# First stage's x pieces: high and low parts of the rows in one 512-column product, a bank per block, halves added by VectorE at eviction

## The chip, the core and the metric

The kernel runs on one core of a Trainium2 chip. The metric is the device time of one execution in microseconds. [...] Each engine works through its own queue in order and meets the others at semaphores.

## The reference

One decoder layer over 2048 rows of width 1024, all in float32: RMSNorm, one input projection, two token mixers side by side, an output projection with residual, RMSNorm, a top-4-of-32 mixture of experts with residual, and a final RMSNorm. What the change touches is the part of the projection that feeds the convolution:

```python
h = rmsnorm(x, norm_mix_w[l])
proj = h @ w_in[l]                       # (2048, 1024) @ (1024, 3096)
q, k, v, g, a_low, z, xbc, dt_raw = jnp.split(proj, split_pts, axis=-1)
...
conv = lax.conv_general_dilated(xbc, ssd_conv_w[l][:, None, :], ...)   # 4 taps, per channel
xbc_act = jax.nn.silu((conv + ssd_conv_b[l]).astype(f32))
```

`xbc` has 1024 channels.

## The kernel before

The first stage, about the first 1030 us, takes the rows in eight rounds of 256 (s = 0 to 7); behind it the experts run in chunks. A float32 product is made of three: each operand is split into a high part (rounded to a narrower format, `fp32r` in the profile) and a low part (the rest), and high x high, high x low and low x high are summed in PSUM. For the rows the parts are `hhi` and `hlo`, for the weights the two halves of each of four buffers of `u2`.

The weights of a round come as 16 units of 1024 x 256 or 512 x 512. Units 0 to 3 are the x pieces (the channels of `xbc`), 4 to 11 the other columns of the input projection, 12 to 15 the output projection. In rounds 0 and 1 the raw unit is loaded, ScalarE makes its high part (`unit_hi`, L989), VectorE its low part (`unit_lo`, L1427), and both are stored to memory, from where later rounds load them ready. A unit's buffer is loaded again four units on, once TensorE is done with it.

An x piece (`x_piece`, L2045 to L2054) computes two blocks of 128 channels over the round's 256 rows. The weights are loaded into TensorE, the rows stream: for each block and each of 8 slices of the width, three products of 256 columns. Both blocks of a piece share one bank, columns 0 to 255 and 256 to 511. Piece n uses bank `pp[n % 2]`: x0 and x2 `pp0`, x1 and x3 `pp1`. `x_out` (ScalarE, L1000; the profile shows the copy under L941) copies the whole bank to `xT`, from where VectorE computes the convolution (`taps`). x2 starts when the copy of x0 is done, x3 when that of x1 is. Between the pieces TensorE does small work of the mixers; in round 0 there is little of it, and x1, x2 and x3 follow each other. After x3 come two small products into `pp0` (the gate step `zz`, L2244), which need the copy of x2, and a small transpose; VectorE then computes `dt0` and `zb` (`dt_zb`, L1532), and after `zb` the first product of unit 4 may start. It needs `pp0` and, for its second half, `pp1`, so the copy of x3.

The order of every engine's work is written out by hand in its `body(s, at)`; `at` is 0, 1, 2, 3 (a loop over rounds 3 to 5), 6 and 7. `rec` holds from round 1, `post` from round 2, `tx` up to round 6, `split` in round 0. `after(engine, step, n)` is a wait, `done` its signal. On ScalarE the copy of x3 follows `norm_sq(a + 3)` (L976), the sum of squares of an x tile that the next round needs and that is loaded during this one.

## Time and profile before

| | us |
|---|---|
| median of 3 runs | 3471.52 (3471.43 to 3477.55) |
| profiled execution, its own time | 3470.43 |
| its span | 3468.8 |
| TensorE busy in the span | 3405.6 (98%) |
| VectorE busy | 2140.4 (62%) |
| ScalarE busy | 1608.0 (46%) |
| x pieces (L2052), share of the chain that ended last | 5% |

The page gives busy time as shares of the span, which is the time from the first to the last instruction. Matmuls overlap: a row's duration is that of one product from start to end, and the pace of a run of them is the distance between starts. The granted clock (PEclk) of TensorE is 1.00 at 2.4 GHz and 0.50 at 1.2 GHz. In a row of the order of time, the number in brackets is how long the engine had stood idle before it, and what released it.

### The profile page before, as it was taken

To read this page: it belongs to the slowest core of one execution; us is meant where nothing else is said; L and a number is where in the kernel's file an instruction comes from. 1 tells how busy PE (TensorE), PEld (TensorE's weight loads), DVE (VectorE), ACT (ScalarE), POOL (GpSimd) and SP (SyncE) were. 2 spreads that over 40 slices of the span, in tenths; PEclk is the share of its full clock that TensorE was granted. 3 is DMA by queue.
4 is the path that set the end of the run, shared out by engine and by line. 5 is a ranking of instruction groups with operands and counts; after the bars stand their busy time and mean duration, and the time that the engine had idled before them with its cause. 6 is when DMAs were issued, how large, how long until landed. Compare 5 with 4: busy or idle time off the path is not lost.

```text
span 3468.8 us, 57452 instructions
## 1 busy us (share of the span) xinstructions
PE 3405.6 (98%) x21623; PEld 3101.2 (89%) x21623; DVE 2140.4 (62%) x2730; ACT 1608.0 (46%) x2045; POOL 630.0 (18%) x848
## 2 busy tenths in 40 slices
PE   7999999999999999999999999999999999999997
PEld 6888888888888999999999999988888888888986
DVE  4555455445456555555566666667777777777777
ACT  4443333333233444444444444455555555555555
POOL 1011111111113111111112112021112112212214
PEclk9999999999999999999999999999999999999998
DMA  9888887887876555555666656667667767767878
GB/s 377 346 321 322 302 288 286 303 300 284 300 254 192 168 165 166 184 182 181 184 192 198 194 181 202 188 206 242 208 212 218 245 214 229 246 223 229 252 241 307
DMA packets 475282, 826.58 MB, mean 238 GB/s; under 512 B 21837, under 2 KB 419293, under 8 KB 458784
## 3 DMA queue, kind: packets, MB, share of 16 engines
q1 hardware_dynamic: 443360, 721.83, 59.4%
q0 software_dynamic: 24320, 75.95, 9.6%
q10 hardware_dynamic: 7488, 27.27, 2.2%
q8 instruction: 73, 1.20, 0.1%
q14 instruction: 41, 0.34, 0.0%
HBM read 726.14 MB, written 98.96 MB: 238 GB/s over the span
## 4 chain that ended last, share of the span: by engine, by line
PE 92%; DMA 2%; DVE 2%; issue 1%; ACT 1%; POOL 0%; SPq 0%; POOLq 0%; DVEq 0%; ACTq 0%
PE pp L2062 14%; PE acc L2483 13%; PE acc L2479 11%; PE acc L2480 10%; PE acc L2481 10%; PE acc L2485 7%; PE pp L2052 5%; PE acc L2495 4%; PE acc L2497 4%; PE acc L2496 4%; PE tpm L2452 2%; PE tp L2031 2%; PE tpm L2458 1%; DMA uraw<-in_w_in 1%; PE seg L2107 1%
## 5 line engine op out<-in xcount | busy, mean ns | idle before, releaser
L1880 DVE TENSOR_TENSOR wlo<-raw,whi 128x2048 fp32r<-128x2048 f32 x384 | 876.0, 2289 | 298.5 <-ACT whi L1287 298.2
L1287 ACT ACTIVATE whi<-raw 128x2048 fp32r<-128x2048 f32 x384 | 730.3, 1910 | 149.1 <-PE acc L2497 102.7
L2483 PE MATMUL acc<-xhl,whi 128*128 128x512 f32 (+3 forms) x2304 | 762.9, 385 | 0.0
L689 POOL TENSOR_TENSOR gate_op<-gate_op 1x1 f32<-1x1 f32 x351 | 169.5, 483 | 2729.1 <-DVE ybuf L1918 533.4
L2485 PE MATMUL acc<-xhl,wlo 128*128 128x256 f32 (+3 forms) x2304 | 624.2, 271 | 0.0
L2479 PE MATMUL acc<-xhl,whi 128*128 128x272 f32 (+3 forms) x1792 | 534.9, 299 | 1.3 <-DVE xhl L1892 1.3
L2480 PE MATMUL acc<-xhl,whi 128*128 128x272 f32 (+3 forms) x1792 | 530.4, 296 | 0.0
L2481 PE MATMUL acc<-xhl,wlo 128*128 128x272 f32 (+3 forms) x1792 | 530.2, 296 | 0.0
L2483 PEld LDWEIGHTS acc<-xhl,whi 128*128 128x128 f32 x2304 | 431.9, 187 | 67.8
L2485 PEld LDWEIGHTS acc<-xhl,wlo 128*128 128x128 f32 x2304 | 437.3, 190 | 0.7
L2479 PEld LDWEIGHTS acc<-xhl,whi 128*128 128x128 f32 x1792 | 336.7, 188 | 1.5 <-issue 1.5
L2480 PEld LDWEIGHTS acc<-xhl,whi 128*128 128x128 f32 x1792 | 336.6, 188 | 0.0
L2481 PEld LDWEIGHTS acc<-xhl,wlo 128*128 128x128 f32 x1792 | 336.5, 188 | 0.0
L2062 PE MATMUL pp<-u,hhi 128*128 128x512 f32 x1024 | 325.8, 399 | 4.2 <-DVE zb L1411 4.2
L2479 PE MATMUL acc<-ahl,whi 128*128 128x272 f32 (+3 forms) x896 | 269.9, 301 | 0.0
L2481 PE MATMUL acc<-ahl,wlo 128*128 128x272 f32 (+3 forms) x896 | 265.4, 296 | 0.0
L2480 PE MATMUL acc<-ahl,whi 128*128 128x272 f32 (+3 forms) x896 | 265.3, 296 | 0.0
L2062 PEld LDWEIGHTS pp<-u,hhi 128*128 128x128 f32 x1024 | 190.3, 189 | 45.0 <-DVE zb L1411 4.3
L2495 PE MATMUL acc<-whi,ahl 128*128 128x512 f32 (+3 forms) x576 | 228.6, 397 | 1.1 <-DVE ahl L1946 1.1
L1320 ACT ACTIVATE ubuf<-acc,bgu 128x256 f32<-128x256 f32 (+7 forms) x200 | 86.6, 470 | 301.0 <-PE acc L2481 193.4
L2497 PE MATMUL acc<-whi,ahl 128*128 128x512 f32 (+3 forms) x576 | 225.3, 391 | 0.0
L2496 PE MATMUL acc<-wlo,ahl 128*128 128x512 f32 (+3 forms) x576 | 225.1, 391 | 0.0
(329 smaller groups left out, 5794.5 us busy)
## 6 DMA issues: line engine op xcount, KB each, us to landing
u<-split_d SPq DMA_DIRECT2D x112, 2048.0 KB, 8.9
raw<-in_moe_w_gate SPq DMA_DIRECT2D x128, 1024.0 KB, 4.8
raw<-in_moe_w_up SPq DMA_DIRECT2D x128, 1024.0 KB, 5.1
raw<-in_moe_w_down SPq DMA_DIRECT2D x128, 1024.0 KB, 9.4
split_d<-u SPq DMA_DIRECT2D x16, 2048.0 KB, 12.7
uraw<-in_w_in SPq DMA_DIRECT2D x12, 1024.0 KB, 10.7
yT<-in_moe_b_down SPq DMA_DIRECT2D x18, 512.0 KB, 12.2
xin<-in_x ACTq DMA_DIRECT2D x14, 512.0 KB, 8.6
```

Source lines behind the costliest of these rows:

```text
L1287: act.activation(whi[:, q % RING, :, :], raw[:, q % RING, :, :], ACT.Copy).then_inc(a_hi, 1)
L1880: dve.tensor_tensor(wlo[:, q % RING, :, :], raw[:, q % RING, :, :], whi[:, q % RING, :, :].bitcast(F32), ALU.subtract).then_inc(v_lo, 1)
L2052: m = pe.matmul(pp[n % 2][:, c * PW:(c + 1) * PW], w_[:, k, c * P:(c + 1) * P], h_[:, k, :], start=(k == 0 and w_ is wh and h_ is hhi), st ...
L2062: m = pe.matmul(pp[t][:, :], h_[:, 4 * q + k, :], w_[:, k, :], start=(q == 0 and k == 0 and h_ is th and w_ is wh), stop=(q == 1 and k == ...
L2479: pe.matmul(into[:, 0:n], hi_, of[:, k, 0, 0:n], start=(k == 0), stop=False)
L2480: pe.matmul(into[:, 0:n], hi_, of[:, k, 1, 0:n], start=False, stop=False)
L2481: m = pe.matmul(into[:, 0:n], lo_, of[:, k, 0, 0:n], start=False, stop=(k == KD - 1))
L2483: pe.matmul(into[:, 0:2 * n].rearrange("p (c n) -> p c n", c=2), hi_, of[:, k, :, 0:n], start=(k == 0), stop=False)
L2485: m = pe.matmul(into[:, n:2 * n], lo_, of[:, k, 0, 0:n], start=False, stop=(k == KD - 1))
L2495: pe.matmul(into, hi_, whi[:, slots_, k, :], start=(k == 0), stop=False)
L2496: pe.matmul(into, hi_, wlo[:, slots_, k, :], start=False, stop=False)
L2497: m = pe.matmul(into, lo_, whi[:, slots_, k, :], start=False, stop=(k == KD - 1))
```

## The change

`hhi` and `hlo` become the two halves of one tensor `hhl` (slice, part, row). One product streams both parts, 512 columns, against the high part of the weights into a whole bank: high x high in columns 0 to 255, low rows x high weights in 256 to 511. A second one of 256 columns adds high rows x low weights to the second half. Each of the two blocks now has a bank, block 0 `pp0`, block 1 `pp1`, in every piece. So a piece is 16 pairs of products in place of 16 triples, and it uses both banks. ScalarE copies the first half of each bank to `xT` (two copies of 256 columns), and VectorE (`x_sum`) adds the second half to it. Each block has steps of its own: x0a and x0, x1a and x1, and so on. A bank is free when VectorE's add is done, and every block of the next piece waits for that; `zz` and unit 4 wait for x3's.

```diff
     "act_sm": ["sm"],
-    "pe_x": ["x0", "x1", "x2", "x3"],
-    "act_x": ["x0", "x1", "x2", "x3"],
+    "pe_x": ["x0a", "x0", "x1a", "x1", "x2a", "x2", "x3a", "x3"],
+    "act_x": ["x0a", "x0", "x1a", "x1", "x2a", "x2", "x3a", "x3"],
+    "dve_x": ["x0a", "x0", "x1a", "x1", "x2a", "x2", "x3a", "x3"],
     "pe_zz": ["zz", "tdt"],
...
             hraw = pa("hraw", [KD, PW])
-            hhi = pa("hhi", [KD, PW], F32R)
-            hlo = pa("hlo", [KD, PW], F32R)
+            hhl = pa("hhl", [KD, 2, PW], F32R)
+            hhi, hlo = hhl[:, :, 0, :], hhl[:, :, 1, :]
             mT = pa("mT", [KD, P])
...
             def x_out(s, n):
-                after(act, f"pe_x.x{n}", s)
-                copy(xT[:, 2 * n:2 * n + 2, TAPS - 1:], pair_cols(pp[n % 2][:, :], 2), f"act_x.x{n}")
+                for c, step in enumerate((f"x{n}a", f"x{n}")):
+                    after(act, "pe_x." + step, s)
+                    copy(xT[:, 2 * n + c, TAPS - 1:], pp[c][:, 0:PW], "act_x." + step)
 
...
 
+            def x_sum(s, n):
+                for c, step in enumerate((f"x{n}a", f"x{n}")):
+                    after(dve, "act_x." + step, s)
+                    tt(xT[:, 2 * n + c, TAPS - 1:], xT[:, 2 * n + c, TAPS - 1:], pp[c][:, PW:], ALU.add, "dve_x." + step)
+
             def h_lo(s):
...
                     mix_ssd(a - 2)
+                x_sum(s, 0)
                 if tx:
...
                     ssd_add(a - 2)
+                x_sum(s, 1)
                 if post:
...
                     gla_decay(b)
+                x_sum(s, 2)
+                if rec:
                     gla_add(b)
+                x_sum(s, 3)
                 dt_zb(s)
...
                     mix_ssd(b)
-                after(dve, "act_x.x3", s)
+                after(dve, "dve_x.x3", s)
                 if rec:
...
 
-            def x_piece(s, n, at):
+            def x_piece(s, n, at, free, count):
 
...
                 wh, wl = unit_of(n, KD)
-                for c in range(2):
+                for c, step in enumerate((f"x{n}a", f"x{n}")):
+                    if free:
+                        after(pe, free[c], count)
+                    both = pp[c][:, :].rearrange("p (v n) -> p v n", v=2)
                     for k in range(KD):
-                        for w_, h_ in ((wh, hhi), (wh, hlo), (wl, hhi)):
-                            m = pe.matmul(pp[n % 2][:, c * PW:(c + 1) * PW], w_[:, k, c * P:(c + 1) * P], h_[:, k, :],
-                                          start=(k == 0 and w_ is wh and h_ is hhi), stop=(k == KD - 1 and w_ is wl))
-                done(m, f"pe_x.x{n}")
+                        pe.matmul(both, wh[:, k, c * P:(c + 1) * P], hhl[:, k, :, :], start=(k == 0), stop=False)
+                        m = pe.matmul(pp[c][:, PW:], wl[:, k, c * P:(c + 1) * P], hhl[:, k, 0, :],
+                                      start=False, stop=(k == KD - 1))
+                    done(m, "pe_x." + step)
 
...
                 after(pe, "dve_h.lo", s)
-                if post:
-                    after(pe, "dve_x2.a1", q)
-                elif rec:
-                    after(pe, "act_in.za", p)
-                x_piece(s, 0, at)
+                x_piece(s, 0, at, ("dve_x2.a1", "dve_x2.b1") if post else ("act_in.za", "act_in.zb") if rec else (),
+                        q if post else p)
                 if tx:
...
                     state(a - 2)
-                if post:
-                    after(pe, "dve_x2.b1", q)
-                elif rec:
-                    after(pe, "act_in.zb", p)
-                x_piece(s, 1, at)
+                x_piece(s, 1, at, ("dve_x.x0a", "dve_x.x0"), s)
                 if rec:
...
                     h2_turned(q * 2, 0)
-                after(pe, "act_x.x0", s)
-                x_piece(s, 2, at)
+                x_piece(s, 2, at, ("dve_x.x1a", "dve_x.x1"), s)
                 if rec:
...
                     gla_state(b, 1, p)
-                after(pe, "act_x.x1", s)
-                x_piece(s, 3, at)
+                x_piece(s, 3, at, ("dve_x.x2a", "dve_x.x2"), s)
                 if rec:
...
                 after(pe, "act_sm.sm", s)
-                after(pe, "act_x.x2", s)
+                after(pe, "dve_x.x3a", s)
                 for c in range(2):
...
                 after(pe, "dve_sp.zb", s)
-                first_half(s, 4, at, of_h, ("dve_sp.zb", "act_x.x3"), s)
+                first_half(s, 4, at, of_h, ("dve_sp.zb", "dve_x.x3"), s)
                 if rec:
...
                     cv_turned(1, p)
```

VectorE, opening round, from the scaling of the rows up to the splits of units 6 to 8, before (`u2` is a weight unit, `pp0` and `pp1` the banks):

```order
L1433 TENSOR_TENSOR hraw<-tp,cols 128x4x128 [waits dve_h,pe_tx,pe_sm,setup_a]
L1433 TENSOR_TENSOR hraw<-tp,cols 128x4x128
L1427 TENSOR_TENSOR u2<-uraw,u2 128x2048 [waits a_uh] x2
L1411 TENSOR_TENSOR dt0<-pm,shr 128x16 [waits pe_zz]
L1411 TENSOR_TENSOR zb<-pp0,shr 128x512
L1427 TENSOR_TENSOR u2<-uraw,u2 128x2048 [waits a_uh] x3
```

And of the changed kernel:

```order
L1435 TENSOR_TENSOR hraw<-tp,cols 128x4x128 [waits pe_tx,dve_h,pe_sm]
L1435 TENSOR_TENSOR hraw<-tp,cols 128x4x128
L1413 TENSOR_TENSOR xT<-xT,pp0 128x256 [waits act_x]
L1413 TENSOR_TENSOR xT<-xT,pp1 128x256 [waits act_x]
L1429 TENSOR_TENSOR u2<-uraw,u2 128x2048 [waits a_uh] x2
L1413 TENSOR_TENSOR xT<-xT,pp0 128x256 [waits act_x]
L1413 TENSOR_TENSOR xT<-xT,pp1 128x256 [waits act_x]
L1413 TENSOR_TENSOR xT<-xT,pp0 128x256 [waits act_x]
L1413 TENSOR_TENSOR xT<-xT,pp1 128x256 [waits act_x]
L1413 TENSOR_TENSOR dt0<-pm,shr 128x16 [waits pe_zz]
L1413 TENSOR_TENSOR zb<-pp0,shr 128x512
L1429 TENSOR_TENSOR u2<-uraw,u2 128x2048 [waits a_uh] x3
```

The adds of x1 stand ahead of the splits of units 4 and 5, those of x2 and x3 behind both.

ScalarE, round 2, from the second part of `qT` (mixer) to `dtl`, before (`xin` is the x tile that is loaded in this round):

```order
L1030 ACTIVATE qT<-tp 64x2x128
L941 ACTIVATE kT<-tp 128x256
L976 ACTIVATE junk,st<-xin 128x1024 [waits d_x,act_sq]
L941 ACTIVATE xT<-pp1 128x2x256 [waits pe_x]
L981 ACTIVATE xin<-xin,st 128x1024 [waits p_norm]
L957 DMA xres<-in_x 128x1024 [waits d_h20,pe_th]
L1120 ACTIVATE dtl<-dt0 128x16 [waits dve_sp]
```

And of the changed kernel:

```order
L1032 ACTIVATE qT<-tp 64x2x128
L942 ACTIVATE kT<-tp 128x256
L977 ACTIVATE junk,st<-xin 128x1024 [waits d_x,act_sq]
L942 ACTIVATE xT<-pp0 128x256 [waits pe_x]
L942 ACTIVATE xT<-pp1 128x256 [waits pe_x]
L982 ACTIVATE xin<-xin,st 128x1024 [waits p_norm]
L958 DMA xres<-in_x 128x1024 [waits d_h20,pe_th]
L1122 ACTIVATE dtl<-dt0 128x16 [waits dve_sp]
```

The copies of x3 are two now, at the same place behind the squares of the x tile.

TensorE, round 2, the end of x3 and the steps behind it, before:

```order
L2052 MATMUL pp1<-hlo,u2 128x256
L2052 MATMUL pp1<-hhi,u2 128x256
L2244 MATMUL pp0<-w_up,smT 128x256 [waits act_x,act_sm,act_rec]
L2244 MATMUL pp0<-w_up,smT 128x256
L2248 MATMUL pm<-ident,smT 128x24 x2
L2137 MATMUL pg<-qT,kT 128x128 [waits dve_g,act_qk]
L2137 MATMUL pg<-qT,kT 128x128 x3
```

And of the changed kernel:

```order
L2066 MATMUL pp1<-hhl,u2 128x512
L2067 MATMUL pp1<-hhl,u2 128x256
L2250 MATMUL pp0<-w_up,smT 128x256 [waits dve_x,act_sm,act_rec]
L2250 MATMUL pp0<-w_up,smT 128x256
L2254 MATMUL pm<-ident,smT 128x24 x2
L2152 MATMUL pg<-qT,kT 128x128 [waits dve_g,act_qk]
L2152 MATMUL pg<-qT,kT 128x128 x3
```

The gate step (`w_up`) waits for VectorE's add of x3's block 0 (`dve_x`) where it waited for ScalarE's copy of x2 (`act_x`).

## Rows read from the trace of the kernel before

**Rows 1.** Busy time by stretch: PE, PEld, DVE, ACT, POOL (count), PEclk, DMA share, GB/s.
```profile
325.00:450.00 125.00, 125.00 (x744) 108.18 (x743) 60.76 (x142) 42.91 (x87) 17.96 (x31) 1.00 0.82 293
```

**Rows 2.** In order of time (start, duration, us): TensorE, x0 of round 5.
```profile
633.56 0.28 PE L2052 MATMUL pp<-hlo,u 128*128 128x256 f32 x1
...
638.95 0.28 PE L2052 MATMUL pp<-hlo,u 128*128 128x256 f32 x1
```

**Rows 3.** In order of time, TensorE, expert stage, pairs 1 and 16.
```profile
2499.63 0.40 PE L2483 MATMUL acc<-xhl,whi 128*128 128x512 f32 x1
2499.87 0.28 PE L2485 MATMUL acc<-xhl,wlo 128*128 128x256 f32 x1
...
2504.93 0.40 PE L2483 MATMUL acc<-xhl,whi 128*128 128x512 f32 x1
```

**Rows 4.** In order of time, TensorE, 512-column products of a row unit.
```profile
583.57 0.39 PE L2062 MATMUL pp<-u,hlo 128*128 128x512 f32 x1
...
588.37 0.40 PE L2062 MATMUL pp<-u,hlo 128*128 128x512 f32 x1
```

**Rows 5.** In order of time, a 256-column copy and a 256-column VectorE operation.
```profile
151.43 0.39 ACT L941 ACTIVATE kT<-tp 128x256 f32<-128x256 f32 x1
...
121.85 0.41 DVE L1411 TENSOR_TENSOR cbm<-pm,m_le 128x256 f32<-128x256 f32 x1
```

**Rows 6.** In order of time, VectorE, opening round.
```profile
56.05 2.29 DVE L1427 TENSOR_TENSOR u<-uraw,u 128x2048 fp32r<-128x2048 f32 x1 [6.39 <-ACT u L989]
58.26 0.17 DVE L1411 TENSOR_TENSOR dt<-pm,shr 128x16 f32<-128x16 f32 x1
```

**Rows 7.** In order of time, ScalarE, opening round.
```profile
48.09 0.60 ACT L941 ACTIVATE xT<-pp 128x512 f32<-128x512 f32 x1 [0.76 <-PE pp L2052]
54.11 1.91 ACT L989 ACTIVATE u<-uraw 128x2048 fp32r<-128x2048 f32 x1 [5.42 <-DMA uraw<-in_w_in]
```

**Rows 8.** In order of time, TensorE, opening round.
```profile
33.10 1.97 PE L2031 MATMUL tp<-ident,xin 128*128 128x128 f32 x8 [3.97 <-ACT xin L981]
...
53.74 1.13 PE L2244 MATMUL pp<-w_up,smT 16*128 16x256 f32 x4
...
59.17 1.19 PE L2062 MATMUL pp<-u,hhi 128*128 128x512 f32 x2 [4.22 <-DVE zb L1411]
```

**Rows 9.** Busy time by stretch, after the two pauses of the opening round.
```profile
36.00:38.00 2.00, 2.00 (x11) 2.00 (x11) 0.49 (x1) 0.00 (x0) 0.00 (x0) 0.50 0.98 410
38.00:39.00 1.00, 1.00 (x9) 1.00 (x8) 0.00 (x0) 0.00 (x0) 0.00 (x0) 0.84 1.03 442
...
62.00:63.00 1.00, 1.00 (x6) 0.80 (x5) 0.00 (x0) 1.00 (x1) 0.00 (x0) 0.89 0.92 387
```

**Rows 10.** The page's DMA issues: KB each, us to landing.
```profile
uraw<-in_w_in SPq DMA_DIRECT2D x12, 1024.0 KB, 10.7
```

**Rows 11.** In order of time, TensorE, the wait for the ramp.
```profile
85.84 3.55 PE L2107 MATMUL seg<-ramp,m_gt 128*128 128x512 f32 x4 [2.33 <-DVE ramp L1411]
```

**Rows 12.** In order of time, ScalarE, round 2.
```profile
267.12 0.60 ACT L941 ACTIVATE xT<-pp 128x512 f32<-128x512 f32 x1 [0.42 <-ACT xres L1062]
...
284.43 1.06 ACT L976 ACTIVATE junk<-xin 128x1024 bf16<-128x1024 f32 x1 [8.76 <-DMA xin<-in_x]
...
285.49 0.58 ACT L941 ACTIVATE xT<-pp 128x512 f32<-128x512 f32 x1
```

**Rows 13.** In order of time, TensorE, round 2, x2's first product and zz.
```profile
267.98 0.36 PE L2052 MATMUL pp<-hhi,u 128*128 128x256 f32 x1
...
280.96 1.12 PE L2244 MATMUL pp<-w_up,smT 16*128 16x256 f32 x4
```

**Rows 14.** In order of time, ScalarE then TensorE, round 6.
```profile
788.32 1.06 ACT L976 ACTIVATE junk<-xin 128x1024 bf16<-128x1024 f32 x1 [2.09 <-DMA xin<-in_x]
789.28 0.19 ACT L976 ACTIVATION_READ_ACCUMULATOR junk<-xin 128x1 f32 x1
...
791.51 1.13 PE L2244 MATMUL pp<-w_up,smT 16*128 16x256 f32 x4
```

## The prediction

> **What bounds the kernel now.** I read the busy time by stretch first, then TensorE's and the other engines' rows in order of time around the x pieces (units 0 to 3 of a round; x0 to x3 below, rounds numbered s = 0 to 7). From round 3 on TensorE never stands still: 125.00 of 125.00 us busy at full clock, with VectorE busy 60.76 and ScalarE 42.91 [rows 1]. There a microsecond of TensorE is a microsecond of the run, and work for the other two is free as long as TensorE never waits for it. The opening round is another stage: TensorE waits for VectorE and ScalarE, which wait for weight units to land and be split [rows 6 to 8]. So three questions decide: how much shorter is a piece, do the new adds come before TensorE wants the bank, and where does a queue ahead of them stand still?
>
> **What the products give.** A piece had 16 triples of 256 columns; between the second product of one x0 and the same product 15 triples later lie 638.95 - 633.56 = 5.39 us, 0.3593 us a triple [rows 2]. It gets 16 pairs, 512 and 256 columns. The expert stage runs this very pair: 15 of them from 2499.63 to 2504.93, 0.3533 us each [rows 3]. That is 0.006 us a pair, 0.10 us a piece. The other bound is built from single forms: 21 products of 512 columns in 588.37 - 583.57 = 4.80 us, 0.2286 each [rows 4], plus a third of the triple, 0.1198, gives a pair of 0.3484 and 0.17 us a piece. I take the pair as it stands in the trace. 24 pieces (rounds 1 and 3 to 7) count, since those of rounds 0 and 2 end in a wait (below): -2.3 us, with -4.2 and 0 as ends.
>
> The Trainium skill, "TensorE: Matmul & The Clock Gate", section "Back-to-back issue gap", gives an isolated matmul columns / 2.4 GHz plus about 2.5 ns. By it dropping one product of three at equal columns saves 2.5 ns a pair, an estimate of 1.0 us for 24 pieces. The trace's 256 columns take 119.8 ns where that rule says 109, so it does not hold here, and the sum would change by 1.3 us only.
>
> **What the evictions cost.** Each piece now has two 256-column copies on ScalarE (such a copy out of PSUM takes 0.39 us, a 512-column one 0.60) and two 256-column adds on VectorE (0.41 us for one that reads PSUM) [rows 5, 7]. That is 64 x 0.39 - 32 x 0.60 = 5.8 us more ScalarE and 64 x 0.41 = 26 us more VectorE over eight rounds, spread over engines half idle [rows 1]: nothing by itself. That the high and low parts of the rows now lie side by side in memory changes no instruction's length or count, and I cost it at nothing. What it moves is the release of the banks. Before, piece n+2 waited for the copy of piece n, a whole piece (5.8 us) in between. Now half c of piece n+1 waits for copy and add of half c of piece n, with one half piece (2.8 us) and the small work between. Copy, add and two hand-overs take about 0.39 + 0.41 + 0.1 = 0.9 us, so in a quiet round it fits. In front of the adds, however, stand whatever VectorE and ScalarE have in their queues.
>
> **Opening round, the first stall.** On VectorE the order is now: adds of x1, splits of units 4 and 5, adds of x2. The split of unit 5 starts at 56.05, released by ScalarE's half of it at 54.11, which waited 5.42 us for the unit to land; it ends at 58.26 [rows 6, 7]. Before, x3 went into the other bank and ran without a pause after x2 (x2's copy is at 48.09 [rows 7], so x2 ends near 47.8). Now x3 needs x2's first add, done at 58.26 + 0.41: it starts at about 58.75 and TensorE has stood 11 us. Behind the late adds queue the decay inputs (dt0, zb) and the splits of units 6 and 7; behind x3 the load of unit 7, which takes its place.
> After such a pause the granted clock is at its lower level (0.50). After 3.97 us of waiting, work resumed at 33.10 and was at half clock until about 38.3; after 4.22 us, from 59.17 to about 62.2 [rows 8, 9]. So 3.0 to 5.2 us at half clock, 1.5 to 2.6 lost. x3: 16 x 0.3533 + 2.1 = 7.75, to 66.5. The small products behind it last from 53.74 to 54.95 (59.17 less its wait), 1.2 us: 67.7. From the start of dt0's row to the first product of unit 4 it took 59.17 - 58.26 = 0.9: 68.6 in place of 59.17, +9.4 [rows 6, 8]. The pause that was there, and its 1.5 us of half clock, go: +8.0 (7.4 to 8.5). Unit 7 is loaded only once x3 is done, at 66.5; 10.7 us to land [rows 10] and some 4 us to be split put it in place at 82, and TensorE, with three units of 5.5 us each (24 x 0.2286) before it, wants it at 85: in time, by 3 us. All later loads of the round are issued as TensorE frees units, so they move along, and so does TensorE's wait for the ramp (2.33 us at 85.84) [rows 11]. Nothing takes the 8 us back, since from round 3 on TensorE has no slack.
>
> **Round 2, the second stall.** ScalarE's copies of x3 stand behind the squares of the next x tile, which waited 8.76 us for its landing, to 284.43; the x3 copy started at 285.49 [rows 12]. That hurt nobody: the next user of pp0, the two-product gate step (zz), needed only x2's copy and ran at 280.96 [rows 13]. Now zz needs x3's first half copied and added: 285.49 + 0.39 + 0.41 + 0.06 = 286.35, +5.4 us, and the pause lowers the clock again, 1.5 to 2.6 us, I take 2.0: +7.4. In the same round x2's first half needs x1's add: copy at 267.12 [rows 12], free at 268.0, against a start at 267.98 [rows 13]: +0.1. In the other rounds with such a tile it lands earlier: in round 6, the tightest, the squares end at 789.47, so bank 0 is free at 790.4, and zz runs at 791.51 [rows 14]; 1.1 us to spare.
>
> **Sum.** 8.0 + 7.4 + 0.1 - 2.3 = +13.2 us. The profiled execution took 3470.43 us (span 3468.8), so 3483.6 by its own time; the median of the runs, 3471.52, lies 1.1 higher: **3484.7 us**. The measurement tells 0.2%, 6.9 us, from no change.
>
> **Rivals.**
> 1. The x tile of round 2 lands in time, over 5.5 us earlier than before. Only the first stall stays: 8.0 - 28 x 0.10 = +5.2, 3476.7. For it: in round 6 that wait is 2.09 us and not 8.76 [rows 14]. Against: the traffic of round 2 is issued by TensorE's own pace and shifts with it.
> 2. Not slower: the pause of round 0 lets the DMA queues get 8 us ahead. It decides from the point where unit 9 and round 2's x tile land some 4 and 6 us sooner after their issue: then the ramp wait (2.3 + 1.5 for its clock) goes and the second stall too: 8.0 - 3.8 - 2.8 = +1.4, 3472.9. Against: the loads are issued only when TensorE frees a place, so there is little to run ahead with.
> 3. The adds never hold TensorE (unit 5's wait absorbed, zz not held): -32 x 0.10 = -3.2, with the other bound -5.6: 3466 to 3468. This would need VectorE to reach x2's adds before 47.8, ahead of a split it has in front of them in its queue; nothing in the trace speaks for it.
> 4. More stalls: tiles landing over 1.1 us later in rounds 3 to 6, where there is as little to spare as in round 6, or half-piece waits that break TensorE's stream 32 times. At 3 us a round for four rounds +12: 3497.
>
> **Chances.** Forecast 0.62 (its own range 3480 to 3489, from 1.1 either way on the clocks, 2 us either way on the landing, 2 on the products); rival 1 0.14, rival 2 0.06, rival 3 0.04, rival 4 0.14. The forecast, rival 4 and the top of rival 1 are slower by over 0.2% (above 3478.5): 0.79. The rest of rival 1 and rival 2 are within it: 0.17. Rival 3 counts as faster: 0.04, though only its far end nears the limit. Range 3476 to 3491: it takes in rival 1 and leaves out rivals 2 and 3 and most of 4.
>
> **What would show it.** In round 0 x3's first product at 58 to 59 us, released by VectorE's add, with the clock at 0.50 behind it; unit 4's first product 9 us later than before. In round 2 a wait of 5 us before the gate step, released by an add. Pieces of about 5.7 us in place of 5.8. From round 3 on every round as long as before less 0.4 us. The forecast is wrong if x3 follows x2 in round 0 without a pause, or if rounds 3 to 7 show waits of TensorE for VectorE.

## The result, and the profile after

In all rows PE is TensorE and PEld its weight loads, ACT is ScalarE, DVE is VectorE, POOL is GpSimd and SP is SyncE; ACTq stands for a transfer (DMA) that ScalarE issues.

The change makes the kernel slower. The median of 4 runs is 3502.66 us (3496.22 to 3509.59), that of the kernel before 3471.69 (4 runs); ratio 1.0087, 95% interval 1.0075 to 1.0099. Forecast were +13.2 us and 3484.7, in a range of 3476 to 3491. The sign was right, the size too small by 18 us. The profiled execution took 3509.59 us (span 3507.9), 39 us more than the profiled one before.

TensorE's three waits that are new or longer in the first stage, in the profile after (engine, tile, line; what it waited for: us in total, times, longest):

```profile
PE pp L2250 <- DVE xT L1413: 12.1, 3, 4.6
PE pp L2066 <- DVE xT L1413: 11.6, 1, 11.6
PE seg L2122 <- DVE ramp L1413: 3.8, 1, 3.8
```

Two of these were forecast, and one of the two came three times: the gate step (L2250) waits for an add in rounds 2, 3 and 4. In order of time, TensorE in the opening round (x3, unit 4, the ramp), in answer to [rows 8, 11]; then the gate step of rounds 1 to 5, in answer to [rows 13, 14]:

```profile
58.48 0.77 PE L2066 MATMUL pp<-hhl,u 128*128 128x512 f32 x1 [11.63 <-DVE xT L1413]
68.88 6.37 PE L2077 MATMUL pp<-u,hhl 128*128 128x512 f32 x27 [0.96 <-DVE zb L1413]
95.61 3.78 PE L2122 MATMUL seg<-ramp,m_gt 128*128 128x512 f32 x4 [3.83 <-DVE ramp L1413]
...
169.28 1.13 PE L2250 MATMUL pp<-w_up,smT 16*128 16x256 f32 x4
297.57 2.04 PE L2250 MATMUL pp<-w_up,smT 16*128 16x256 f32 x4 [4.57 <-DVE xT L1413]
433.72 2.07 PE L2250 MATMUL pp<-w_up,smT 16*128 16x256 f32 x4 [3.42 <-DVE xT L1413]
570.71 2.07 PE L2250 MATMUL pp<-w_up,smT 16*128 16x256 f32 x4 [4.15 <-DVE xT L1413]
703.29 1.13 PE L2250 MATMUL pp<-w_up,smT 16*128 16x256 f32 x4
```

In rounds 6 and 7 the gate step stands at 830.40 and 956.45, with no wait. The distance between gate steps is the length of a round. In the kernel before they stand at 157.10, 280.96, 408.61, 536.26, 663.92, 791.51 and 918.24 in rounds 1 to 7:

| | to round 1 | 1 to 2 | 2 to 3 | 3 to 4 | 4 to 5 | 5 to 6 | 6 to 7 |
|---|---|---|---|---|---|---|---|
| before | 157.10 | 123.86 | 127.65 | 127.65 | 127.66 | 127.59 | 126.73 |
| after | 169.28 | 128.29 | 136.15 | 136.99 | 132.58 | 127.11 | 126.05 |
| difference | +12.2 | +4.4 | +8.5 | +9.3 | +4.9 | -0.5 | -0.7 |

They sum to +38.2 of the 39 us. A wait lengthens the round that ends with it, and what it costs afterwards falls into the next one. The windows behind the wait of round 4 show why (from:to, length, busy time of PE, PEld, DVE, ACT and POOL with counts, granted clock of TensorE, DMA share, GB/s):

```profile
568.00:570.00 2.00, 0.00 (x0) 0.00 (x0) 0.00 (x0) 1.22 (x3) 0.00 (x0) 0.78 0.87 328
570.00:572.00 2.00, 1.29 (x3) 1.10 (x4) 0.75 (x2) 1.38 (x3) 0.89 (x3) 0.50 1.00 369
576.00:578.00 2.00, 2.00 (x11) 2.00 (x11) 0.00 (x0) 0.00 (x0) 0.00 (x0) 0.50 0.08 31
580.00:582.00 2.00, 2.00 (x6) 1.52 (x6) 1.30 (x3) 0.62 (x1) 0.00 (x0) 0.50 0.00 0
582.00:584.00 2.00, 2.00 (x9) 1.59 (x8) 1.22 (x3) 0.71 (x3) 0.00 (x0) 0.81 0.00 0
584.00:586.00 2.00, 2.00 (x11) 1.63 (x10) 0.30 (x1) 0.00 (x0) 0.00 (x0) 1.00 0.00 0
```

A wait of 4.15 us, and TensorE, busy all the time afterwards, runs at 1.2 GHz until about 583. What it does there are the small products behind the gate step, at half speed:

```profile
572.86 2.08 PE L2152 MATMUL pg<-qT,kT 128*128 128x128 f32 x8
574.73 3.46 PE L2197 MATMUL pm<-rw,mT 128*128 128x32 f32 x16
578.00 1.95 PE L2043 MATMUL tp<-ident,mixed 128*128 128x128 f32 x8
```

In the kernel before, at full clock in the same round:

```profile
537.41 1.16 PE L2137 MATMUL pg<-qT,kT 128*128 128x128 f32 x8
538.40 1.87 PE L2182 MATMUL pm<-rw,mT 128*128 128x32 f32 x16
540.11 1.07 PE L2031 MATMUL tp<-ident,mixed 128*128 128x128 f32 x8
```

What made the waits of rounds 3 and 4 is in ScalarE's rows. After, round 3 and then round 4: the expert-stage input of the second token tile (`xres`, L1064), which waits until the store of that tile (`xacc_d<-xres`) is done, behind it the issue of the x tile, then the squares, which wait for its landing, and in round 4 the two copies of x3 behind them:

```profile
415.11 1.15 ACT L1064 ACTIVATE xres<-xres,sto 128x1024 f32<-128x1024 f32 x1 [6.12 <-DMA xacc_d<-xres]
...
417.05 0.37 ACTq L946 DMA_DIRECT2D xin<-in_x  x1
...
431.79 1.06 ACT L977 ACTIVATE junk<-xin 128x1024 bf16<-128x1024 f32 x1 [6.63 <-DMA xin<-in_x]
...
548.74 1.15 ACT L1064 ACTIVATE xres<-xres,sto 128x1024 f32<-128x1024 f32 x1 [3.37 <-DMA xacc_d<-xres]
...
550.70 0.36 ACTq L946 DMA_DIRECT2D xin<-in_x  x1
...
568.78 1.06 ACT L977 ACTIVATE junk<-xin 128x1024 bf16<-128x1024 f32 x1 [7.35 <-DMA xin<-in_x]
569.74 0.19 ACT L977 ACTIVATION_READ_ACCUMULATOR junk<-xin 128x1 f32 x1
569.84 0.64 ACT L942 ACTIVATE xT<-pp 128x256 f32<-128x256 f32 x2
```

And in the kernel before, round 4:

```profile
519.44 0.42 ACTq L945 DMA_DIRECT2D xin<-in_x  x1
532.26 1.06 ACT L976 ACTIVATE junk<-xin 128x1024 bf16<-128x1024 f32 x1 [1.25 <-DMA xin<-in_x]
```

In round 4 the squares begin 18.1 us after the issue where it was 12.8, and the issue itself comes 1.0 us later ahead of the gate step. In round 3 the larger part is the issue. The kernel before issued that tile at 391.79, 16.8 us ahead of its gate step; after, it is issued 13.3 us ahead of the moment at which the gate step would have run without its wait (433.72 - 3.42), because `xres` in front of it waited 6.12 us for its store where it had waited 2.41. From issue to squares it then took 14.7 us, which was 13.0 before. So the tile comes late in two ways: its issue stands behind another transfer in ScalarE's queue, and its own landing takes longer. I had read the spare time of all later rounds from the one landing of round 6 [rows 14]. The trace before already had more than one value, 13.0, 12.8, 12.5 and 13.8 us in rounds 3 to 6, and 17.3 in round 2.

### The profile page after: what moved, and what is told of

It is laid out like the page before. It is cut to its first block, busy times and chain, and to the rows that moved or that the text cites. A ratio compares the mean times of both kernels' runs of the same rounds, so it can differ in the third digit from the quotient of the medians.

```text
span 3507.9 us, 56534 instructions
## 1 busy us (share of the span) xinstructions
PE 3424.2 (98%) x21111; PEld 3093.7 (88%) x21111; DVE 2165.8 (62%) x2794; ACT 1612.2 (46%) x2077; POOL 641.0 (18%) x848
## 4 chain that ended last, share of the span: by engine, by line
PE 89%; DMA 5%; DVE 3%; issue 1%; ACT 1%; POOL 0%; SPq 0%; ACTq 0%; POOLq 0%; DVEq 0%
PE pp L2077 13%; PE acc L2489 13%; PE acc L2485 10%; PE acc L2486 10%; PE acc L2487 10%; PE acc L2491 6%; PE acc L2501 4%; PE acc L2503 3%; PE acc L2502 3%; PE pp L2066 2%; PE tpm L2458 2%; PE tp L2043 1%; DMA xin<-in_x 1%; DMA xacc_d<-xres 1%; DMA uraw<-in_w_in 1%
## 5 line engine op out<-in xcount | busy, mean ns | idle before, releaser
L690 POOL TENSOR_TENSOR gate_op<-gate_op 1x1 f32<-1x1 f32 x351 | 186.5, 531 | 2761.2 <-DMA xacc_d<-ybuf,tabb 521.1
L2077 PE MATMUL pp<-u,hhl 128*128 128x512 f32 x1536 | 374.2, 401 | 1.0 <-DVE zb L1413 1.0
L2077 PEld LDWEIGHTS pp<-u,hhl 128*128 128x128 f32 x1536 | 290.5, 191 | 63.8 <-issue 2.9
```

Source lines behind the costliest of these rows:

```text
L690: pool.tensor_tensor(gate_op[0:1, 0:1], gate_op[0:1, 1:2], gate_op[0:1, 1:2], ALU.add).then_inc(gate_ran, 1)
L2077: m = pe.matmul(pp[t][:, :], h_[:, 4 * q + k, :], w_[:, k, :], start=(q == 0 and k == 0 and h_ is th and w_ is wh), stop=(q == 1 and k == ...
```

## The experiments

Each kernel was compared with runs of the kernel before on the same chip (medians of that one: 3476.21 beside e1 to e4, 3474.03 beside e5 to e8, 3472.72 beside e9 to e11, 3475.68 beside e12). The theories are these. Theory of the queues: all of the loss is TensorE waiting for adds and copies that stand behind other work in the queues of VectorE and ScalarE, and the low clock behind each wait. Rival: the adds, the finer hand-over and their PSUM traffic cost by themselves.

| kernel | us | ratio to before, 95% |
|---|---|---|
| e1_x2_adds_first | 3487.33 | 1.0029 (1.0018 to 1.0039) |
| e2_x3_half_first | 3488.02 | 1.0034 (1.0020 to 1.0047) |
| e3_both | 3483.04 | 1.0020 (1.0011 to 1.0029) |
| e4_gate_wait_alone | 3494.74 | 1.0056 (1.0040 to 1.0071) |
| e5_x3_ahead | 3472.08 | 0.9993 (0.9984 to 1.0002) |
| e6_x1_ahead_too | 3471.39 | 0.9994 (0.9985 to 1.0003) |
| e7_all_orders | 3467.68 | 0.9982 (0.9973 to 0.9991) |
| e8_no_adds | 3468.87 | 0.9992 (0.9983 to 1.0001) |
| e9_before_orders | 3471.09 | 0.9997 (0.9988 to 1.0007) |
| e10_ramp_ahead | 3464.82 | 0.9981 (0.9972 to 0.9990) |
| e11_before_ramp_ahead | 3468.62 | 0.9989 (0.9980 to 0.9998) |
| e12_opening_as_changed | 3481.40 | 1.0016 (1.0007 to 1.0025) |

### x2's adds ahead of the split of unit 5

```diff
                 if split:
                     unit_lo(4)
-                    unit_lo(5)
...
                 x_sum(s, 2)
+                if split:
+                    unit_lo(5)
```

> Changed kernel with one edit: in the opening round VectorE adds x2's halves ahead of the split of unit 5. Theory (the loss is two kinds of waits of TensorE, each with its stretch at half clock): the 11.6 us wait before x3 goes; the gate step now waits for x3's add, which stands behind that split, so first products of unit 4 start near 61 us in place of 68.9. About 8 to 10 us less than the changed kernel's 3502.7, near 3493; the waits of the gate step in rounds 2 to 4 stay. Rival (64 adds and the traffic they make slow every round a little): under 2 us gained.

Measured 1.0029. In the profiled run x3's wait of 11.6 us is 2.83, but round 2 keeps its stall, and round 7 has one of another kind: x2 waits for x1's add, whose copy stands on ScalarE behind work that waits for a transfer (`xacc_d`).

```profile
49.93 0.47 PE L2067 MATMUL pp<-hhl,u 128*128 128x512 f32 x1 [2.83 <-DVE xT L1413]
...
288.11 2.04 PE L2251 MATMUL pp<-w_up,smT 16*128 16x256 f32 x4 [5.77 <-DVE xT L1413]
...
919.25 0.77 PE L2067 MATMUL pp<-hhl,u 128*128 128x512 f32 x1 [4.33 <-DVE xT L1413]
```

So every place where an add or copy follows a transfer in a queue is a place where TensorE can now stall.

The gain was twice what I expected. The kernel is 11.1 us slower than the one before, where the change as it stands is 31.0 slower: 20 us gained by an edit of the opening round alone, 8 to 10 expected. The expectation said that the waits of rounds 3 and 4 stay. In this profile they are gone (rounds 3 to 6 show no wait at the gate step), though ScalarE's order, the products and the adds are as in the changed kernel, and though round 2 stalls for longer, 5.77 us. So a stall in round 2 does not by itself bring those of rounds 3 and 4. In round 3 the tile is again issued late, 13.8 us ahead of the gate step, but its squares begin 10.3 us after the issue, where it was 14.7. The stalls of rounds 3 and 4 hang on the landing as much as on the issue, and one edit elsewhere was enough to lose them. The gains of the edits can therefore not be added up.

### The first half of x3 ahead of the squares; and both edits

```diff
+                x_out(s, 3, (0,))
                 if tx:
...
                     norm_sq(a + 3)
-                x_out(s, 3)
+                x_out(s, 3, (1,))
```

> Changed kernel with one edit: ScalarE copies the first half of x3 ahead of the squares of the x tile that it waits for, in every round. Theory: the gate step never waits for VectorE's add in rounds 2 to 6, each such wait with the stretch at half clock behind it is gone: near 3479 to 3482 us, 20 less than the changed kernel, and runs that differ less from each other. The opening wait of 11.6 us stays, with some 9 us of cost against the kernel before. Rival (the adds themselves): no more than 4 us gained.

> Both edits, of the opening round and of the gate step. Theory: only the shorter products stay, 0.4 to 0.6 us a round in seven rounds, against some 1.5 us of the gate step's wait in the opening round: 3468 to 3471 us, level with the kernel before (3471.7) or up to 0.1% faster. Rival (adds and copies cost by themselves): 3480 us or more.

Measured 1.0034 and 1.0020. The first gains 19 us against the change as it stands, close to the 20 expected. Both together are a miss: level with the kernel before was expected, and at 6.8 us slower the number is the one that the rival had named. The profile tells why. The gate step no longer waits for the tile, but in round 2 the wait moves a few products on: VectorE's add of x3's second half waits for the copy behind the squares, and dt0 is queued behind that add. In both runs TensorE stands over 3 us in round 2, and the clock falls again. Both edits together, TensorE and then VectorE:

```profile
289.92 3.52 PE L2200 MATMUL pm<-rw,mT 128*128 128x32 f32 x16 [3.35 <-DVE dt L1415]
```

```profile
289.36 0.42 DVE L1415 TENSOR_TENSOR xT<-xT,pp 128x256 f32<-128x256 f32 x1 [6.92 <-ACT xT L942]
289.70 0.17 DVE L1415 TENSOR_TENSOR dt<-pm,shr 128x16 f32<-128x16 f32 x1
```

From round 2 to 3 it takes 133.85 us, then 126.87, 126.86 and 127.02. The loss is one wait that the edit left in place, in round 2, and not a little in every round.

### The gate step's wait alone, in the kernel before

```diff
-                after(pe, "act_x.x2", s)
+                after(pe, "act_x.x3" if at >= 2 else "act_x.x2", s)
```

> Kernel before with one edit: from round 2 on the gate step waits for ScalarE's copy of x3 and not of x2; products, banks and evictions as before. Theory: the copy stands behind the squares of the late x tile, so round 2 has a wait of some 5 us before the gate step and over 10 us at half clock behind it, 9 to 11 us of cost, and rounds 3 and 4 may follow as they did in the changed kernel: 3481 to 3500 us. Were the later waits (rounds 3 and 4) due to the new products or the adds, only round 2 shows one and the time is near 3481. Rival (the wait is harmless, the clock comes back at once): 3476 us.

Measured 1.0056, +18.5 us, with no other part of the change in it, in the range expected. The profiled run, gate steps of rounds 2 to 4:

```profile
287.93 2.04 PE L2244 MATMUL pp<-w_up,smT 16*128 16x256 f32 x4 [5.61 <-ACT xT L941]
421.45 1.13 PE L2244 MATMUL pp<-w_up,smT 16*128 16x256 f32 x4 [0.69 <-ACT xT L941]
549.87 1.13 PE L2244 MATMUL pp<-w_up,smT 16*128 16x256 f32 x4 [0.69 <-ACT xT L941]
```

From round 2 to 3 lie 133.52 us, where a round is 127.65 before. The wait in round 3 accounts for 0.69, so 5.2 us were lost after the wait was over. Windows of the same run, behind the wait of round 2 and in round 5:

```profile
290.00:292.00 2.00, 2.00 (x12) 1.96 (x10) 0.77 (x2) 1.44 (x4) 0.00 (x0) 0.50 0.59 234
...
298.00:300.00 2.00, 2.00 (x8) 1.59 (x8) 0.59 (x2) 1.34 (x3) 0.00 (x0) 0.79 0.00 0
300.00:302.00 2.00, 2.00 (x11) 1.65 (x10) 1.45 (x3) 0.00 (x0) 0.00 (x0) 1.00 0.00 0
...
680.00:684.00 4.00, 4.00 (x27) 4.00 (x26) 1.68 (x8) 1.47 (x3) 0.00 (x0) 0.64 0.98 412
684.00:688.00 4.00, 4.00 (x13) 3.32 (x12) 2.42 (x7) 1.34 (x3) 0.00 (x0) 0.51 0.40 166
```

From the end of the wait at 287.9 to about 299 it is at half clock. The short waits of 0.69 us mostly cost their own length: round 3 to 4 takes 128.42, 0.77 more than before. But in round 5, behind such a short one, the clock fell too, for part of 680 to 688, and that round took 131.66, 4.1 more. It fell again behind the short wait of round 7 (0.50 from 942 to 946). So the low clock here belongs to a late gate step, but not only to waits of several us.

Of the three stalls only that of round 2 comes back here. The expectation had left it open whether rounds 3 and 4 follow, and taken one large wait alone as a sign that those two come from the products or the adds. The kernel e1_x2_adds_first speaks against that: it has the products and the adds, and no stall in rounds 3 and 4 either. What e4 shows is the price of a wait at this place, 5.61 us and 5.2 of clock, without anything else of the change.

### Both copies of x3 ahead; x1 and the x tile ahead too; the adds left out

```diff
+                x_out(s, 3)
                 if tx:
...
                     norm_sq(a + 3)
-                x_out(s, 3)
```

(with the edit of x2's adds). The second kernel adds, on ScalarE:

```diff
                 if post:
-                    for t in range(2):
-                        h2_of(q, t)
-                        h2_out(q, t)
+                    h2_of(q, 0)
+                    h2_out(q, 0)
                 x_out(s, 1)
                 if tx:
                     x_in(a + 3)
+                if post:
+                    h2_of(q, 1)
+                    h2_out(q, 1)
```

The third is the first without `x_sum`, every `dve_x` wait turned into `act_x`; the sum of the halves is left out.

> The changed kernel with VectorE's adds of x2 ahead of the split of unit 5 (opening round) and both of ScalarE's copies of x3 ahead of the squares of the x tile (all rounds). Theory of the queues (all of the loss is TensorE waiting behind other work in the queues of VectorE and ScalarE, and the half clock behind each wait): the first half of this order, with only one copy moved, left one wait in round 2 (logits, 3.4 us) and a pitch 133.85 from round 2 to round 3 against 127.65; with both copies moved that wait goes, every round from 3 on is 0.5 to 0.7 us shorter than before, and the run is within 2 us of the kernel before. Rival (the adds or the shared banks cost TensorE by themselves, through half pieces that wait and PSUM traffic): the loss stays at +5 or more though no wait over 1 us is left in rounds 2 to 7.

> As the kernel with x3's copies ahead, and in ScalarE's queue x1's copies and the load of the x tile stand ahead of the second token tile's expert-stage input (h2_of of tile 1), which waits for a transfer. Theory of the queues: the x tile's load is issued within 0.3 us of its place coming free in every round (it was 3.5 us in rounds 2 and 3), so that its landing no longer varies, and the scatter between runs shrinks to that of the kernel before (6 us between fastest and slowest, at most); 0 to 2 us faster than the kernel with x3's copies ahead. Rival (the landing varies with the DMA queues and not with the issue): no difference in time, and the squares still wait 6 us or more for the tile in round 2; since nobody waits behind them any more this costs nothing either.

> The kernel with x3's copies ahead, with VectorE's 64 adds left out (the low parts of the product are computed by TensorE and never added) and with all waits on the adds turned into waits on ScalarE's copies. What it measures is the price of the adds and of the hand-over to VectorE. Theory of the queues: only in the opening round does TensorE wait for an add, so this is 1 to 4 us faster than the kernel with x3's copies ahead, and from round 3 on each round is as long as there. Rival (the adds cost by themselves, through PSUM traffic or short waits at each half piece): each round is 0.5 us or more shorter here, 5 us or more in all.

Measured 0.9993, 0.9994 and 0.9992. With x3's copies out of the tile's way, and x2's adds ahead of the split, the loss of 31 us is gone. The adds cost nothing that can be measured: 64 adds more or less change the time by less than some 4 us. Round 3 to 4 and 4 to 5 take 126.97 and 126.87 us with them, 126.87 and 126.87 without. At 0.5 us or more a round the rival falls. Moving x1 and the tile too did not change the time: in one profile it took away a wait of 1.8 us in round 3 (round 2 to 3: 128.97, then 126.87), and the scatter did not shrink (7.5 us and 8.9 us from fastest to slowest), against what I expected.

### All orders in the opening round

```diff
                 if split:
+                    x_sum(s, 2, (0,))
                     unit_lo(4)
-                    unit_lo(5)
+                    x_sum(s, 2, (1,))
...
                 x_sum(s, 3)
                 dt_zb(s)
                 if split:
+                    unit_lo(5)
```

(ScalarE's copies likewise.)

> As the kernel with x1's copies ahead too, and in the opening round the copies and adds of x2 and x3 and the decay inputs (dt0, zb) stand ahead of the split of unit 5 (x2's first half ahead of that of unit 4). Theory of the queues: x3 follows x2 with a pause of under 3 us, the gate step behind it; unit 4's first product starts near 55.6 in place of 59.17 in the kernel before, and 5 us ahead of the kernel with x1's copies ahead; whether unit 5 then comes in time decides what of that is kept: between -5 and -1 us against the kernel before, 3471 to 3475 if that one is at 3476. Rival: the splits of units 4 to 7 and their stores move back by as much, unit 5 is waited for, and the gain against the kernel with x1's copies ahead is under 1 us.

Measured 0.9982 (0.9973 to 0.9991): faster than the kernel before by 3 to 9 us, by 6.4 in the medians where 1 to 5 was expected. x3 follows x2 with no wait of note, unit 4 starts at 54.83 where it was 59.17 [rows 8]; the ramp's wait is longer than before, 5.84 us in place of 2.33 [rows 11], and takes part of it back.

```profile
54.83 5.46 PE L2083 MATMUL pp<-u,hhl 128*128 128x512 f32 x23 [0.96 <-DVE zb L1417]
...
84.86 3.78 PE L2128 MATMUL seg<-ramp,m_gt 128*128 128x512 f32 x4 [5.84 <-DVE ramp L1417]
```

The same run, x0 of round 5, to be held against [rows 2]:

```profile
630.28 0.28 PE L2073 MATMUL pp<-hhl,u 128*128 128x256 f32 x1
...
635.49 0.28 PE L2073 MATMUL pp<-hhl,u 128*128 128x256 f32 x1
```

15 pairs in 5.21 us, 0.3473 each, against 0.3593 a triple: 0.19 us a piece and 0.77 a round, which is what the rounds show (126.87 against 127.65).

### Controls, and the ramp

The kernel before with the same orders (x tile and x1's copy, x3's copy, dt0 and zb ahead of the split of unit 5); then both, in the opening round, with:

```diff
                 if split:
+                    ramps(a, 0, s)
                     unit_lo(9)
```

> The kernel before with the same orders of the queues: the x tile's load and x1's copy ahead of h2_of of tile 1, x3's copy ahead of the squares, the decay inputs (dt0, zb) ahead of the split of unit 5. It tells what the orders alone are worth without the change. Theory (the 6 us that the changed kernel with all orders has over the kernel before come from the products, about 0.75 us in each round, and the orders only give back what the change lost): pitch of rounds 3 to 6 stays at 127.6, unit 4's first product comes 2 to 3 us earlier than 59.17, and this is 0 to 3 us faster than the kernel before (ratio 0.9992 to 1.0000). Rival (the gain is that of the orders, the products give nothing): as fast as the changed kernel with all orders, ratio 0.998 or less.

> The changed kernel with all orders, and in the opening round VectorE makes the ramp ahead of its split of unit 9, which waits 4.2 us for ScalarE; the ramp's inputs are ready before. Theory of the queues: TensorE's wait for the ramp (5.84 us at 84.86) goes, the segment products start near 79, unit 9 becomes the next thing that is late or just in time (its split ends at about 84); 3 to 6 us faster than with all orders alone, ratio to the kernel before 0.9965 to 0.9975. Rival (the opening round is set by the landing of its weight units, and a wait removed comes back before the next unit): round 1 starts no more than 1 us earlier, ratio as with all orders (0.9982).

> The kernel before with its new orders (x tile, x3's copy, decay inputs) and the ramp ahead of the split of unit 9: the control of the changed kernel with the ramp ahead. If the orders and the change are independent, the pair differs by the products alone, 4 to 6 us (0.0012 to 0.0017 of the time), with this one the slower. If the shorter pieces are only taken back by waits for units, the pair is equal within 1 us.

Measured 0.9997, 0.9981 and 0.9989. The orders alone give the kernel before nothing that can be told. With the orders as nearly equal as the two kernels allow, the changed kernel is ahead by 0.0015 (5 us) in one pair and by 0.0008 (3 us) in the other; the uncertainty of such a difference is some 0.0013 (4.5 us), so the first is just clear of it and the second is not. Both agree with the 0.77 us a round of the rows. For the changed kernel the ramp's edit is a miss: the wait for the ramp is gone and its products start 5 us earlier, at 79.61, but the next one in line is late in its place,

```profile
97.65 1.09 PE L2050 MATMUL tp<-ident,e 128*128 128x128 f32 x4 [3.46 <-DVE e L1417]
```

and round 1 begins only 0.8 us earlier. The opening round's rival holds there. The kernel before did gain from the same edit, 2.5 us in the medians (0.9997 to 0.9989), and its round 1 begins 2.5 us earlier, at 126.75 in place of 129.26; the gain in time is within the uncertainty.

### The opening stall alone

The kernel with x1 and x3 ahead, without the edit of x2's adds.

> The changed kernel with VectorE's queue as the change left it (adds of x2 behind the splits of units 4 and 5), and only ScalarE's order mended (x1's and x3's copies and the x tile's load moved ahead), so that no round from 2 on waits. It tells what the stall of the opening round costs alone: x3 at 58.5 released by VectorE's add after a wait of about 11 us, as in the changed kernel. Theory (the opening stall is +8 to +12.6 us, and all rounds from 3 on are 0.78 us shorter): round 3 and later pitches 126.87, and the run is 3 to 7 us slower than the kernel before, ratio 1.0009 to 1.0020; against the kernel with the adds of x2 also moved (ratio 0.9994) it is 5 to 9 us slower. Rival (the pause lets units land ahead and round 1 takes most of it back): less than 3 us slower than that kernel, ratio 1.0003 or less.

Measured 1.0016, 5.7 us slower than the kernel before as expected. Against the kernel that differs in the edit alone (0.9994) it is 0.0022 or 7.6 us, give or take some 4. That other kernel is not free of opening waits itself (1.86 us before x3, 2.85 before the gate step), so this is less than the whole stall. The profiled run:

```profile
58.87 0.77 PE L2070 MATMUL pp<-hhl,u 128*128 128x512 f32 x1 [10.84 <-DVE xT L1416]
68.44 6.87 PE L2081 MATMUL pp<-u,hhl 128*128 128x512 f32 x22 [0.96 <-DVE zb L1416]
```

From round 2 on there is no wait for an add, and rounds 3 to 5 take 126.87 us.

## Why the prediction fell short

- **Opening stall: right in mechanism, place and start, somewhat small in size.** Forecast: x3 at 58.75, unit 4 at 68.6; after: 58.48 and 68.88. It was priced at 8.0 us. The kernel with this stall alone is 5.7 us slower than the kernel before although its pieces are 4.6 us shorter in sum, so it costs about 10, give or take 3. Its gate step of round 1 is 10.6 us late, and 12.2 in the profile after. The weak step was "so does TensorE's wait for the ramp" (moves along, unchanged). In the profile after that wait grew to 3.83 us from 2.33, which takes back the 1.5 us of half clock that had gone at unit 4, and behind it the clock stayed at half through 96 to 104, while it was back by 90 before. In the profile of the kernel with the stall alone that wait kept its length, 2.28 us.
- **Round 2: the wait was right, its clock was the mis-sized term.** Forecast 5.4 + 2.0. Measured 4.57 of waiting, and in the round that follows some 5.9 of clock: 136.15 is 8.5 above 127.65, of which 3.42 is the next wait, and the products give 0.8 back. The same sum gives 6.0 and 5.7 behind the waits of rounds 3 and 4, and the kernel with the gate wait alone 5.2. I had taken the time at half clock from the opening round, where the clock is back 3.0 to 5.2 us after the pause [rows 8, 9]. Behind the gate step it was at half clock for 11 to 13 us. What TensorE does differs between the two places: there products of 256 and 512 columns follow at once or after eight small ones, here small products stand for some 9 us. That this makes the difference was not tried.
- **"In the other rounds such a tile lands earlier ... 1.1 us to spare": this step failed, and it is the largest part.** Rounds 3 and 4 stalled as well, 3.42 + 6.0 and 4.15 + 5.7 us: 19 us in the profiled run. This was rival 4's mechanism, given 0.14 and priced at 3 us a round, where a round costs 9 to 10. Neither the issue nor the landing of the tile keeps its place: in round 3 it was issued 3.6 us later ahead of the gate step and landed 1.7 us slower, in round 4 1.0 us later and 5.3 slower (18.1 us where it was 12.8). Moving the copies off that path takes all of it away.
- **Products: the other bound was nearer.** Forecast 0.10 us a piece, measured 0.19, against the 0.17 of the bound built from single forms. Over 24 pieces 4.6 us in place of 2.3. By the rule for an isolated matmul in the Trainium skill, "TensorE: Matmul & The Clock Gate", section "Back-to-back issue gap", one product less at equal columns saves about 2.5 ns, an estimate. In this stream of products it saved 12 ns a pair (0.3593 - 0.3473), and the measurement decides.
- **Adds at nothing by themselves: right within some 4 us**, as the kernel without the adds shows. The copies were not left out in any kernel.
- Rivals 1 to 3 (the tile in time, DMA ahead, adds never waited for) did not happen as the change stands. "From round 3 on every round as long as before less 0.4 us" holds for the rounds that no wait touches, with 0.5 to 0.8.

The profiled run's +38.2 us is made of 12.2 to round 1, 12.1 of gate-step waits, 17.5 of clock behind them (what is left of those rounds' lengths), less 3.6 of shorter products (0.1 from round 1 to 2, three times 0.78, then 0.5 and 0.7). The median of the runs is 7 us lower than that execution. Against the forecast of 13.2 the largest missing part of it is the 19 us of rounds 3 and 4, then 4 each for the clock behind the wait of round 2 and for the opening; the wait of round 2 was 0.8 shorter, and the products gave 1.3 more up to round 7. The sign was no luck: both stalls of the forecast are in the trace.

Open: why the tile took 18.1 us to land in round 4 and 13.5 in round 5, and why the store of `xres` took 12.9 us from issue to the end of the wait for it in round 3, where it had taken 9.6. The weight units of 2048 KB are in another queue (SyncE's) than the tile, but all transfers share the 16 DMA engines; their busy share between issue and squares was 0.96 in round 4 after, 0.98 in round 5 and 0.93 in round 4 before, which does not tell the long landing from the short ones. Only one execution of the changed kernel has a trace, the slowest of the four (3496 to 3510, mean clock 0.986 against 0.988 and 0.989). The others are 7 to 13 us faster, about the price of one stall, so I take it, as an estimate, that they had one stall less; which one is not known.

## What to carry to other kernels

Giving a hand-over one more engine ties the tensor engine to everything in front of it in two queues: go through both queues, in every round, for whatever waits for a transfer, and move the new work ahead of that first. A spare time of 1 us read from one landing is no spare time where the landing spreads over 5 us, and the issue of that transfer can itself stand behind another transfer. And price a wait in a saturated stage at its length plus the half clock behind it, taken from rows of that very place where there are any: here 4 us of waiting cost 9 to 10. Once the queue orders were mended, the change was worth 3 to 9 us against the kernel before.

## What was not expected of the hardware

The clock can fall with no pause at all. In the kernel with the ramp ahead, behind the gate step of round 2, TensorE waits for nothing and is at 1.2 GHz for over 3 us:

```profile
280.00:281.00 1.00, 1.00 (x12) 1.00 (x10) 0.69 (x2) 0.00 (x0) 0.87 (x3) 1.00 1.04 422
281.00:282.00 1.00, 1.00 (x10) 1.00 (x10) 0.47 (x1) 0.98 (x1) 0.00 (x0) 0.94 0.90 385
282.00:283.00 1.00, 1.00 (x6) 1.00 (x7) 0.11 (x1) 0.97 (x4) 0.00 (x0) 0.50 1.11 475
284.00:285.00 1.00, 1.00 (x5) 0.90 (x4) 0.92 (x3) 0.00 (x0) 0.00 (x0) 0.50 1.02 434
286.00:287.00 1.00, 1.00 (x6) 0.82 (x5) 0.01 (x1) 0.96 (x1) 0.00 (x0) 1.00 0.78 320
```

From round 2 to 3 that run took 128.56 us, where 126.87 is usual. The same came once more in that run, behind the gate step of round 5: TensorE waits for nothing, the clock is 0.50 from 665 to 667, and that round took 128.57. It falls where the small products stand, the place at which it stayed low for so long behind a wait, and fell in rounds 5 and 7 of the kernel with the gate wait alone. Part of the scatter of all these kernels may come from it; that was not tried.
